# First V group through SBUF, and row dots placed elsewhere, in a hybrid decoder step

## The reference, cut to what matters

```python
q = (tb @ w_q).reshape(PEER_BLOCK, PEER_HEADS, 2, PEER_HALF)
s = jnp.einsum('thik,hink->thin', q, sub_keys)
s_top, i_top = lax.top_k(s, PEER_TOPK)                 # 16 of 128 for each half
cand = s_top[:, :, 0, :, None] + s_top[:, :, 1, None, :]
best_s, best_c = lax.top_k(cand, PEER_TOPK)            # 16 experts for each head
...
# for each token: sum over its 8*16 experts e of softmax(best)[e] * gelu(h . u[e]) * v[e]
```

## Time and profile before

| | us |
|---|---|
| median of 3 runs (lowest, highest) | 2330.66 (2328.43, 2336.01) |
| the profiled execution's own time | 2328.26 |
| its span | 2326.5 |
| TensorE busy, share of the span | 2260.8, 97% |
| VectorE busy | 1623.5, 70% |
| GpSimd busy | 1435.6, 62% |
| ScalarE busy | 809.8, 35% |

### The profile page before, as it was taken

How to read it: one execution, slowest core, us unless ns; L and a number is a source line. 1 busy time by engine, 2 the same in 40 slices (tenths; PEclk the granted TensorE clock), 3 DMA queues, 4 the chain that set the end, 5 groups by cost and what they waited for, 6 DMA issues and landing times.

```text
span 2326.5 us, 39113 instructions
## 1 busy us (share of the span) xinstructions
PE 2260.8 (97%) x14926; PEld 2185.2 (94%) x14926; DVE 1623.5 (70%) x2826; ACT 809.8 (35%) x1186; POOL 1435.6 (62%) x851
## 2 busy tenths in 40 slices
PE   9999999999999999999999989999969999999998
PEld 8999999987899999999999989999869999999998
DVE  7865444446688236067899999999477777777774
ACT  4433222431232012133443434444334444444442
POOL 5554433442354555546877857676777888888873
PEclk9999999999999999999999989999989999999999
DMA  5224223236753233237988969999998999999982
GB/s 211 87 77 143 91 95 100 93 116 210 262 187 105 86 125 95 82 121 262 304 302 295 317 205 288 288 311 302 335 381 329 373 371 366 363 367 372 379 325 81
DMA packets 212803, 535.23 MB, mean 230 GB/s; under 512 B 16816, under 2 KB 101168, under 8 KB 210224
## 3 DMA queue, kind: packets, MB, share of 16 engines
q1 hardware_dynamic: 111392, 234.65, 31.5%
q0 software_dynamic: 46080, 167.79, 19.2%
q10 hardware_dynamic: 55184, 130.77, 15.2%
HBM read 453.89 MB, written 79.25 MB: 229 GB/s over the span
## 4 chain that ended last, share of the span: by engine, by line
PE 82%; DVE 10%; POOL 3%; DMA 2%; issue 1%; ACT 1%; DVEq 0%; SPq 0%; ACTq 0%; POOLq 0%
PE ps L948 44%; PE ps L684 28%; PE ps L1004 3%; POOL w_lo L658 2%; DMA ug<-rows_u,eid 1%; POOL ug L650 1%; DVE ug L1989 1%; DVE prev L1788 1%; PE ps L961 1%; PE ps L861 1%; PE ps L848 1%; DMA cxb<-parked_tiles 1%; PE ps L856 1%; PE ps L865 1%; PE ps L881 1%
## 5 line engine op out<-in xcount | busy, mean ns | idle before, releaser
L629 POOL TENSOR_SCALAR w_hi<-raw 128x1024 fp32r<-128x1024 f32 x129 | 138.2, 1071 | 517.0 <-issue 387.1
L658 POOL TENSOR_TENSOR w_lo<-raw,e_hi 128x1024 fp32r<-128x1024 f32 x128 | 319.1, 2493 | 149.7 <-PE ps L948 142.0
L658 POOL TENSOR_TENSOR w_lo<-raw,w_hi 128x1024 fp32r<-128x1024 f32 x128 | 318.3, 2488 | 121.5 <-PE ps L948 117.9
L948 PE MATMUL ps<-p_hi,w_lo 128*128 128x416 f32 x1024 | 361.9, 353 | 0.0
L948 PE MATMUL ps<-g_hi,w_lo 128*128 128x416 f32 x1024 | 360.3, 352 | 0.0
L631 POOL TENSOR_TENSOR w_lo<-raw,w_hi 128x1024 fp32r<-128x1024 f32 x129 | 320.1, 2481 | 10.8
L684 PE MATMUL ps<-h_hi,w_hi 128*128 128x288 f32 (+2 forms) x1216 | 274.0, 306 | 1.8 <-ACT ma L1279 1.8
L684 PE MATMUL ps<-h_lo,w_hi 128*128 128x288 f32 (+2 forms) x1216 | 262.2, 297 | 0.0
L684 PE MATMUL ps<-h_hi,w_lo 128*128 128x288 f32 (+2 forms) x1216 | 261.8, 297 | 0.0
L1989 DVE CUSTOM_DVE_ANT_0 ug<-ug,ps 128x1024 f32<-128x1024 f32 x160 | 192.0, 1212 | 64.1 <-DMA ug<-rows_u,eid 48.9
L1998 DVE SCALAR_TENSOR_TENSOR ps<-ug,coef,ps 128x1024 f32<-128x1024 f32 x158 | 203.7, 1289 | 29.8 <-DVE x L2138 25.2
(11 more groups left out here) (359 smaller groups left out, 5185.3 us busy)
## 6 DMA issues: line engine op xcount, KB each, us to landing
raw<-units SPq DMA_DIRECT2D x385, 512.0 KB, 4.3
gate_scratch<-gt SPq DMA_DIRECT2D x52, 512.0 KB, 7.1
activation_scratch<-ge ACTq DMA_DIRECT2D x120, 208.0 KB, 5.0
abuf<-activation_scratch ACTq DMA_DIRECT2D x30, 832.0 KB, 8.5
gbuf<-gate_scratch ACTq DMA_DIRECT2D x30, 832.0 KB, 12.0
prev<-ssm_in ACTq DMA_DIRECT2D x8, 1024.0 KB, 6.7
ssm_s<-prev ACTq DMA_DIRECT2D x8, 1024.0 KB, 4.5
cxb<-parked_tiles ACTq DMA_DIRECT2D x8, 870.0 KB, 6.4
```

Source lines behind the costliest of these rows:

```text
L629: pool.tensor_scalar(w_hi[:, s, :], raw[:, r, :], 1.0, 1.0, ALU.mult, ALU.mult).then_inc(s_whi, 1)
L658: pool.tensor_tensor(w_lo[:, n % 2, :], raw[:, n % RAW, :], e_hi[m % HS_].bitcast(F32), ALU.subtract)\
L948: last = mm(accp[par], w[:, k * P:(k + 1) * P], x_[:, k, t0:t0 + ND], start=k == 0 and i == 0, stop=k == KT - 1 and i == 2)
```

## The change

Four things move.

1. Row dots: 84 to 76 in the search, 44 to 68 behind the one-hots (two or three a block), 32 to 16 at the turn, 4 of them ahead. Rows 128 to 143 are dotted in the blocks from block 20 on, so the spread columns are turned into `h_rows` behind the units of block 20, and a second time into `h_spread` behind the first unit of the last block.
2. The first seven gathers stand behind units 13, 14 and 15 (3, 2, 2) and not all behind 13.
3. Gelu of units 120 to 127 goes to `abuf` in SBUF. `act_part` copies each part to `prod` later: parts 0 and 1 in the step of unit 123, two a step in those of 124 and 125, one in each of 126 and 127. The loads of gates for group 0 are issued before unit 119's Gelu, those of acts and gates for group 1 all behind `expert_gate(7)`.
4. The gate stores of block pair 11 are issued one or two units sooner.

The diff, cut to its core:

```diff
-DOTS_T = [0, 24, 24, 24, 12]
-DOTS_B = [2 - (b % 3 == 2) for b in range(NB)]
-D_LEAD = 12
+DOTS_T = [0, 22, 22, 22, 10]
+B_ROWS = 20
+DOTS_B = [3 - (b % 5 in (1, 3)) if b < B_ROWS else 3 - (b % 3 == 0) for b in range(NB)]
+D_LEAD = 4
...
-    if m == UT[0] + 1:
-        return range(UG)
+    first = UT[0] + 1
+    if first <= m < first + len(UG_FIRST):
+        return range(sum(UG_FIRST[:m - first]), sum(UG_FIRST[:m - first + 1]))
...
+                    if b == NB - 1 and m == M_BLOCK[b]:
+                        pe.wait_ge(s_gt, NB)
+                        turn_rows(2, spread_rows, h_spread)
+                if b == B_ROWS:
+                    pe.wait_ge(s_ud, N_PICK)
+                    turn_rows(1, spread_rows, h_rows)
...
-                    act.wait_ge(s_ud, N_PICK)
-                    if u >= 2:
-                        act.wait_ge(s_p, u - 1)
-                    act.activation(prod[u % 2], accp[par], ACT.Gelu).then_inc(s_accf[par], 1)
+                    act.activation(abuf[:, u // 4, u % 4, :], accp[par], ACT.Gelu).then_inc(s_accf[par], 1)
...
                 expert_hi(TAIL + u + HS_)
-                if u:
-                    hi_part(0, u - 1, 0)
+                if u == 3:
+                    act.wait_ge(s_ud, D_TAIL)
+                    act_part(0, 0, True)
+                    act_part(0, 1, True)
+                if u == GI - 1:
+                    act_part(0, u, True)
+                for i in range(max(2 * u - 8, 0), 2 * u - 6):
+                    hi_part(0, i, 0)
+                    if i + 2 <= u:
+                        act_part(0, i + 2, True)
...
-            hi_part(0, GI - 1, 0)
             act.wait_ge(s_pm, GI)
-            load_gates(1, 1)
+            for hb in range(2):
+                load_half(1, hb)
...
+            expert_gate(0)
             for u in range(GI):
-                expert_gate(u)
+                if u + 1 < GI:
+                    expert_gate(u + 1)
...
-                if u:
-                    expert_low(u - 1)
-                if u + 1 < GI:
-                    for k in tail_dots(u):
-                        row_dot(k)
+                expert_low(u)
+                for k in tail_dots(u):
+                    row_dot(k)
```

More of the change, by code:

```diff
@@ L67 @@
 UG = 7
+UG_FIRST = [3, 2, 2]
+assert sum(UG_FIRST) == UG
 PICK_LAG = 4
@@ L71 @@
 N_ROW = N_PICK + N_PICK // SPREAD
-DOTS_T = [0, 24, 24, 24, 12]
-DOTS_B = [2 - (b % 3 == 2) for b in range(NB)]
-D_LEAD = 12
+DOTS_T = [0, 22, 22, 22, 10]
+B_ROWS = 20
+DOTS_B = [3 - (b % 5 in (1, 3)) if b < B_ROWS else 3 - (b % 3 == 0) for b in range(NB)]
+D_LEAD = 4
 D_TAIL = sum(DOTS_T) + sum(DOTS_B)
-assert D_TAIL == N_PICK
+assert sum(DOTS_T) + sum(DOTS_B[:B_ROWS]) == N_PICK
 TAIL = NKEYS - GI
@@ L124, with store_after @@
 N_TURNED = len(TT) - 1 if ND > T_HALF else len(TT) - 2
+def store_after(B, i):
+    left = NB // 2 - 1 - B
+    return 6 + i * 3 // GQ if left > 1 else 5 + i // 2 if left else 6
 def pair_half(B):
@@ L158, in gathers_after @@
 def gathers_after(m):
-    if m == UT[0] + 1:
-        return range(UG)
-    return [j + UG for j, (_, c) in enumerate(ROWS) if max(c + ROW_LAG, UT[0] + 2) == m and j + UG < len(ROWS)]
+    first = UT[0] + 1
+    if first <= m < first + len(UG_FIRST):
+        return range(sum(UG_FIRST[:m - first]), sum(UG_FIRST[:m - first + 1]))
+    return [j + UG for j, (_, c) in enumerate(ROWS)
+            if max(c + ROW_LAG, first + len(UG_FIRST)) == m and j + UG < len(ROWS)]
 def trunk(nc, xT, x_rows, units, keys, cols, heads, hist_a, hist_s, ssm_in, rows_u, rows_v,
@@ L581, in _ @@
                     for i in range(GQ):
-                        if n == U_PEER + M_BLOCK[2 * B + 1] + 6 + (i * 3 // GQ if B + 1 < NB // 2 else 0):
+                        if n == U_PEER + M_BLOCK[2 * B + 1] + store_after(B, i):
                             store_gates(B, i)
@@ L965, in turn_rows @@
             def turn_rows(i, columns, out):
-                pe.wait_ge(s_gp, i + 1)
+                pe.wait_ge(s_gp, min(i, 1) + 1)
                 for k in range(KT):
@@ L1457, in _ @@
                     activated(m)
-            for m in range(M_GATE, TAIL):
-                activated(m)
             def load_acts(g, hb):
@@ L1470, in load_gates @@
                     .then_inc(s_gl[hb], 16)
+            act.wait_ge(s_gs[0], 16 * GQ * (NB // 4))
+            act.wait_ge(s_gs[1], 16 * GQ * ((NB // 2 - 1) // 2))
+            for hb in range(2):
+                load_gates(0, hb, NB // 2 - 1)
+            for m in range(M_GATE, TAIL):
+                activated(m)
             def load_half(g, hb):
@@ L1475, in load_half, with act_part @@
                 load_gates(g, hb)
-            def act_part(g, u):
-                if u % 4 == 0:
+            def act_part(g, u, first=False):
+                if u % 4 == 0 and not first:
                     act.wait_ge(s_al[u // 4], g * 16)
-                act.wait_ge(s_p, g * GI + (u - 1))
+                if first:
+                    act.wait_ge(s_accf[(L0 + u) % 2], (L0 + TAIL + u) // 2 + 1)
+                if not first or u >= 2:
+                    act.wait_ge(s_p, g * GI + (u - 1))
                 act.activation(prod[u % 2], abuf[:, u // 4, u % 4, :], ACT.Copy).then_inc(s_ap, 1)
@@ L1504, in _ @@
                     act.wait_ge(s_as[1], 8 * TAIL)
[L1505 to L1509, removed]
-            hi_part(0, GI - 1, 0)
+                    act.wait_ge(s_gs[1], 16 * GQ * (NB // 4 + 1))
             act.wait_ge(s_pm, GI)
-            load_gates(1, 1)
+            for hb in range(2):
+                load_half(1, hb)
             act.wait_ge(s_ud, N_ROW)
@@ L1988, in row_dot @@
                 rows = row_landed(k)
-                dve.tensor_tensor_reduce(rows, rows, h_rows if k < N_PICK else h_spread, 1.0, 0.0, ALU.mult, ALU.add, dots[:, k:k + 1])\
+                dve.tensor_tensor_reduce(rows, rows, h_rows if k < D_TAIL else h_spread, 1.0, 0.0, ALU.mult, ALU.add, dots[:, k:k + 1])\
                     .then_inc(s_ud, 1)
@@ L2143, in expert_gate @@
                 g, u = divmod(i, GI)
[L2144 to L2148, removed]
+                dve.wait_ge(s_ap, i + 1)
                 if u % 4 == 0:
@@ L2160, in expert_low @@
                     .then_inc(s_p, 1)
+            expert_gate(0)
             for u in range(GI):
[L2163 to L2164 removed]
+                if u + 1 < GI:
+                    expert_gate(u + 1)
+                if u == 1:
                     for i in range(2):
                         dve.wait_ge(s_gs[i], 16 * GQ * ((NB // 2 + i) // 2))
[L2167 to L2174 removed]
+                expert_low(u)
+                for k in tail_dots(u):
+                    row_dot(k)
             dve.wait_ge(s_act, 1)
```

15 lines of the change are left out of this document (6 added, 9 removed).

## The result

The changed kernel takes **2363.12 us** (median of 4 runs, 2360.09 to 2365.55) against 2332.18 for the kernel before: ratio 1.0132, 95% interval 1.0111 to 1.0153, about 31 us slower. The forecast was 2350, in a range of 2312 to 2366, so the time lies inside the range, 3 us from its upper edge. The profiled execution took 2365.55, its span is 2363.8. In short: rows of the blocks were gathered too late for their dots, and TensorE waited for what stands behind these dots.

The account below looks back on a forecast made before the run. VectorE was taken as full from 1380 to 1650 us, and MatrixE as bound by a few long waits. Search -16, blocks +35 and turn 0 gave +19 on 2328.26: 2347.3 profiled, 2350 as a median, range 2312 to 2366.

Parts of the forecast that it names:

- Blocks, +35: Blocks: 24 more dots, nine gathers behind the unit where their row is due; +35 us, bounds +4 and +50.
- The wait worked out from row 88: Block 6: MatrixE waits for one-hots behind row 88's late gather, 3.0 us, or 6.1 with a slower landing and second split.
- the working's bias: Blocks: 5 us taken off because the same working of before gives about 1 us less slack than its rows.
- The dots fit: Faster rival: VectorE's stretch shrinks by most of what dots add, rows land near 5.8 us; blocks +4, total 2310; chance 0.22.
- Only the full engine costs: No-change rival: rows in time, but 27.4 us of dots on the full engine cost 11 to 14; 2328; chance 0.12.
- Late once, VectorE has no idle time to catch up in: Blocks: after a late row the full VectorE cannot recover; five full places at 5.2 us counted, 26 us.
- Search, -16: Search: eight dots fewer and the 4.72 us stall gone give -13.2, clock -2.8; together -16 us.
- the arrival at gates(0): End of search: MatrixE reaches gates(0) at 1362.9, not 1367.6, and waits about 2.4 us there.
- The term for the clock: Search: the clock had not yet fallen 2.4 us into the old wait, so gates(0) saves 2.8 us.
- Turn, 0: Turn: new waits and half clock of 27.0 us replace the 27.4 lost before; 0, bounds -15 and +8.
- The chains: Turn: MatrixE waits 7.6 us for unit 125, 3.0 before unit 127, 0.8 at V unit 0, 9.0 for group 1's loads.
- the earlier gates' load and the stores of the last pair: Turn: both move one or two units with MatrixE behind neither, 0 us; a late store would show first in GpSimd's splits.

Follow-up runs that it names:

- run 1: Changed kernel without the row gathers for rows 76 to 143, VectorE's instructions kept, output not the reference's: 2329.29 us, 0.9989 of the kernel before.
- run 2: Changed kernel with gathers into slots that the blocks' rows leave placed one unit sooner in GpSimd's list: 2336.08 us, 1.0026 of the kernel before.
- run 3: Changed kernel with gathers into slots that the blocks' rows leave placed two units sooner in GpSimd's list: 2328.19 us, 0.9993 of the kernel before.
- run 5: Kernel before, no dots added, gathers of the blocks three units later so 29 rows lead their use by 1 unit: 2341.41 us, ratio 1.0046.
- run 6: Kernel before, no dots added, the same gathers four units later so 29 rows have a lead of 0: 2426.09 us, ratio 1.0411.
- run 4: Changed kernel with the loads of group 0's gates back behind the Gelu of unit 120: 2363.59 us, 1.0138 of the kernel before.
- run 10: run 9 with the last pair's four gate stores one behind each of four loads of raw: 2306.58 us, 0.9902 of the kernel before.
- run 9: run 3 plus group 1's first-half loads behind expert_gate(3) and eleven dots ahead of the first gated unit, slots refilled from unit 121: 2310.36 us, 0.9913.

## Why the prediction was right, and where it was off

The direction, the mechanism and most of the places were right; the median was 13 us low. The sum was +19 against +37.3 between the profiled executions, and it was too low in every stage that the change touches. That the forecast gave gates(0) at 1365 us and the trace shows 1365.32 is luck: the first stretch was 2.3 us shorter, and from the first U unit on the start came 2.5 us later than forecast.

- *Blocks, +35 against +42.7.* The late rows are the cause (runs 1 to 3, 5, 6). The wait worked out from row 88, 3.0 to 6.1 us, was 4.76 when it came. Mis-sized were the count, six long waits and not five, and the clock behind each, 2.0 us (12.0 / 6) and not 1.6. Short waits were 1.5 us, not 5, and the 5 us taken off for the working's bias should not have been taken. These last two errors nearly cancel, 3.5 us too many against 5 too few, which was luck too.
- *The rivals.* "The dots fit" had its physics right, and the rule of the Trainium skill (SBUF — State Buffer, Who interferes with whom) that a VectorE instruction with one input in PSUM leaves GpSimd free is borne out: dots of 1.21 to 1.22 us in the mean in every run, the same beside a split or not, and 1.6 us for 24 more of them in run 1. It lost as the text said, since a gather behind a unit does not come sooner. "Only the full engine costs" had put 11 to 14 us on these dots, which run 1 shows to be about 2. "Late once, VectorE has no idle time to catch up in" is right in the words and wrong as a condition: run 6 makes the same waits with 44 dots. The lead decides whether there are waits. Whether denser dots make each late row dearer these runs do not part: 84 us for 29 rows at a lead of 0 in run 6, 42.7 us for nine (and eleven at 1) in the changed kernel.
- *Search, -16 against -10.7.* The step that failed is the arrival at gates(0). TensorE stood there 9.45 us and at half clock again (5.28 us), where 2.4 at full clock were expected. TensorE itself came sooner than I had taken it to, at 354.3 us after the first U unit and not at 359.1 (1362.9 in the forecast; 363.8 in the kernel before): with the wait of 4.72 three shorter ones for `w_lo` and the half clock behind them went. VectorE came later than I had taken it to, 10.7 us sooner than before and not 13.2. It had the 9.1 us of eight dots and 7.4 us of waits for rows (15.1 us now, 22.5 in the earlier trace rows) less to do, and gave some 6 us back (16.5 less 10.7). No row of mine had covered the other instructions of the search, and which of them lie beside a split of GpSimd changed with the timing. One line, 1001 to 1370 us, shows how much that can be:

```profile
L2091 DVE TENSOR_TENSOR pick<-best,sm 128x128 f32<-128x128 f32 (+1 forms) x5 | 3.1, 616 | 0.2
```

and after the change:

```profile
L2111 DVE TENSOR_TENSOR pick<-best,sm 128x128 f32<-128x128 f32 (+1 forms) x5 | 9.5, 1908 | 0.2
```

  Three of these five instructions now lie beside a split and take 3.0 us each, one did before (2.0 us), and the others take 0.2 to 0.3. A copy of the same search went the other way (`keyd`, four of 128x8, 7.2 to 0.8 us in all), so this line is an example and not the account. The term for the clock would not have held either: in run 3 a wait of 2.34 us ahead of unit 123 was followed by a granted clock of 0.50 (1673 to 1675 us), and that unit took 6.2 us and not 4.5.

- *Turn, 0 against +4.7, and 2.9 behind it.* The chains came as worked out, to within 0.3 us: 7.33 us for `w_lo` ahead of unit 125 (7.6 forecast), 2.82 ahead of 127 (3.0), 0.74 in V unit 0 (0.8), 9.00 ahead of V unit 2 (9.0). GpSimd stood 12.76 us ahead of gather 155, waiting for the dot of row 148. That is the first of the following rows, one each of GpSimd, SP, ScalarE and TensorE; the other three are of what comes next:

```profile
1727.56 0.96 POOL L661 DMA_INDIRECT ug<-rows_u,eid  x1 [12.76 <-DVE dots L2009]
...
1686.61 13.48 SPq L581 DMA_DIRECT2D gate_scratch<-gt  x4
...
1711.29 1.06 ACT L1389 ACTIVATE e_hi<-raw 128x1024 fp32r<-128x1024 f32 x1 [12.26 <-DMA raw<-units]
...
1712.90 0.69 PE L959 MATMUL ps<-g_hi,w_hi 128*128 128x416 f32 x1 [5.76 <-ACT abuf L1410]
```

The step that failed costed the earlier gates' load and the stores of the last pair at nothing. Those four stores took 13.5 us of SP's time (6.0 in the kernel before), ScalarE waited 12.26 us for raw, and unit 123 started 5.76 us late, where 2.4 ahead of unit 124 had been expected. The text had said that a late store would show in the splits; it showed in ScalarE's conversion, one engine sooner, and the Gelu behind it. Both halves of the step count: run 4, with the gates' load moved back, brings the stores to 7.3 us and takes this wait away, though the 2.3 us forecast ahead of unit 124 then appear and the median stays; run 10 brings it down by the place of the stores. That they came late through the blocks' waits is not what made them long: with the blocks on time they took 13.3 us in run 3 and 12.6 in run 1. The other term that was too small is the clock. The ten units of the stretch lost 77.7 - 45.6 = 32.1 us, of which the waits are 25.7 and half clock behind them 6.5, where the sum had 2.8 for it. The 2.9 us lie behind V unit 2: 1.4 of them in the next two units, which took 10.53 us and not 9.15, half clock behind the 9.0; the rest is within what the runs differ by (589.8 to 592.8).

## What to carry to other kernels

When work is put where an engine has room, ask first when its data arrives: a ring of slots refilled at fixed places has a lead, it shrinks when the use gets denser, and at zero lead each refill stands in series with the engine that sets the places. Here the place of the issues was worth 39 us and the 24 instructions 2. And count what a queue must issue in one piece: four stores of 512 KB in a row held a load of the same size behind them for 17.4 us, where they cost 1.9 us apart.

## What the runs showed that I had not expected

- The step from a lead of one unit to none: 7.5 us to 84 us in the blocks (runs 5 and 6).
- The issue of one gate store on SP, the last of the four, took 11.2 us in run 9, with the DMA engines full (share 1.06 to 1.07 at 1650 to 1670 us), against 0.43 to 0.53 when the stores stood apart (run 10). Full engines alone do not make it: the last store of run 10 took 0.47 us at 1666.47, at a share of 1.06 (1665 to 1670 us). In run 9 the first two of the four took 0.43 and 0.58 us, the third 5.0.
- The same code ahead of the first U unit took 999.5 to 1007.7 us in the different executions, a spread of 8 us and several times what some experiments were to tell. Medians of 4 to 10 runs and a cut by stretches were both needed.
- Dots shortened their neighbours: one-hot products in the blocks went from 1.80 to 1.63 us in the mean (run 3, 194.4 us for 119) when 24 dots were put between them. 63 of that run's 69 dots in the window lay beside a split, and only 47 products did, against 74 before.
